# Turning the rotated keys and queries through memory, with all such transfers issued by GpSimd

## The chip, the cores and the metric

The kernel runs on one core of a Trainium2 chip. The metric is the device time of one execution in microseconds; lower is better. The core's engines run side by side, each working through its own list of instructions in order, and wait for one another on semaphores: TensorE (PE in the profile, PEld its weight loads) multiplies matrices and transposes 128x128 tiles, VectorE (DVE), ScalarE (ACT) and GpSimd (POOL) do elementwise work, SyncE (SP) issues the loads of the weights. Sixteen DMA engines move the data, whoever issues a transfer.

## The reference

One layer of an encoder for 256 tokens of width 2048, in float32. The part around the change is the attention branch: keys (4 heads) and queries (16 heads) of 128 channels are normalised per head, rotated, and used in a softmax over all tokens.

```python
q = rms_norm(q.reshape(b, s, ATTN_Q_HEADS, ATTN_HEAD_DIM), q_norm_g[layer])
k = rms_norm(k.reshape(b, s, ATTN_KV_HEADS, ATTN_HEAD_DIM), k_norm_g[layer])
v = v.reshape(b, s, ATTN_KV_HEADS, ATTN_HEAD_DIM)
q = apply_rope(q, cos, sin)
k = apply_rope(k, cos, sin)
y_attn = gqa_bidir_blocks(q, k, v)
...
branch_a = y_ssm @ w_ssm_up[layer]
branch_b = y_attn @ w_attn_up[layer]
merged = jax.nn.sigmoid(gate_a) * branch_a + jax.nn.sigmoid(gate_b) * branch_b
x = x + merged @ w_out[layer]
h2 = rms_norm(x, g_mlp[layer])
x = x + jnp.square(jax.nn.relu(h2 @ w_mlp_in[layer])) @ w_mlp_out[layer]
```

## The kernel before

The whole layer is a list of windows, written out in `walk`. A window multiplies the 256 tokens (two blocks of 128) by a 2048x512 slice of a weight matrix, in eight pieces p = 0 to 7 of 256 rows each. Every float32 product is made in three passes of a rounded high part and a low remainder, so a piece is 12 TensorE instructions of 512 columns. For each piece SyncE loads 128x1024 values into `raw`, ScalarE makes the high part `whi` (L653), VectorE the low part `wlo` (L1087), and TensorE uses both. `raw`, `whi` and `wlo` are rings of four pieces. ScalarE runs up to three pieces ahead of TensorE, VectorE two.

Behind each piece stands side work of the windows before, named in the last argument of `window(...)`: `rope` for a window of keys or queries, `attend` for the attention of one key head, and so on. Each engine has its own function of that name, called with the piece number p, and does its share in the order of the list, after its share of the piece. So whatever waits in a side function also holds up the high or low part of the following pieces on the same engine.

Several results have tokens in the partitions and are needed with channels in the partitions: they must be turned. Ten of these turns (four of `z`, three of `merged`, three of `residual`) go round TensorE: VectorE transposes 32x32 blocks into `blocks` (`turn_blocks`, L1125), ScalarE issues one transfer to the scratch rows `block_rows` in memory (`put_blocks`, L676), waits until it has landed and issues four transfers back into `turned_to` (`get_blocks`, L686), which place the blocks. ScalarE then makes the high part and VectorE the low part (`split_high`, `split_low`). Keys and queries go over TensorE instead: `rope` n = 0 is the keys and n = 1 to 4 the four groups of four query heads. At p = 6 TensorE waits for the rotated values in `tmp_a` and transposes eight tiles into the PSUM tensor `S` (`transpose_round`, L1834); at p = 7 ScalarE copies them as `kT_hi` or `qT_hi` (L919) and VectorE makes `kT_lo` or `qT_lo` (L1459).

The rotation itself takes VectorE and GpSimd: squares on ScalarE (L913), their sums on VectorE (L1428, L1431), an inverse root on GpSimd (L1716), the scaling on VectorE (L1440), then at p = 3 four multiplications by sines on GpSimd (L1770) and at p = 4 and 5 the multiplications by cosines and the additions on VectorE (L1451, L1454).

The windows around the change stand so in `walk`; (10, 1) and the like name a window by its row and half:

```python
window(10, 1, "v", 0, [("zturned", 3), ("rope", 0)])
window(11, 0, "q", 0, [("values", 0)])
window(11, 1, "q", 1, [("rope", 1)])
window(12, 0, "q", 2, [("rope", 2)])
window(12, 1, "q", 3, [("rope", 3)])
window(13, 0, "ssm_up", 0, [("attend", 0), ("rope", 4)])
window(13, 1, "ssm_up", 1, [("attend", 1), ("gated_a", 0)])
```

Within `attend` each of four heads h goes round all engines: scores on TensorE at p = h, maximum on VectorE, exponential on ScalarE, division on VectorE at p = h + 1 (L1475), transposes of the probabilities on TensorE at p = h + 3 (L1977), their high part `pT_hi` on ScalarE (L944) and low part `pT_lo` on VectorE (L1480) at the same p, and the product with the values on TensorE one piece later (L1813 to L1815, `S<-pT_hi,vg_hi`).

Of the kernel before, what the change touches and what calls it, by code (L numbers as in the profile page):

```python
# [65 lines left out]
BLOCK_ROUNDS = [rnd for rnd in range(TS_END) if rnd not in ON_PE]  # L66
# [3 lines left out]
def walk(eng, window):  # L70
# [194 lines left out]
def build(nc, x, x_t, w_in, w_dt, gains_in, taps_in, rows_in, w_ssm_up, w_attn_up, w_out, w_mlp_in, w_mlp_out,  # L265
# [129 lines left out]
    rden = place("rden", [P, 4, TB])  # L395
    assert top[0] <= nc.sbuf_usable_end, (top[0], nc.sbuf_usable_end)
# [3 lines left out]
    turned_to = nc.alloc_sbuf_tensor_at("turned_to", [P, 4, 4, TB, Q], F32, offset=region_r + 4 * TB * N)  # L400
    channels = nc.alloc_sbuf_tensor_at("channels", [P, 4, T], F32, offset=region_r + 8 * TB * N)
# [67 lines left out]
    r_sq, r_v, r_root, r_t, r_made = sem("r_sq"), sem("r_v"), sem("r_root"), sem("r_t"), sem("r_made")  # L469
# [82 lines left out]
    turned_wide = turned_to[:, :, :, :, :].rearrange("p i c b t -> p (c b) i t")  # L552

# [94 lines left out]
    def _(act):  # L648
# [22 lines left out]

        def put_blocks(rnd):

            d = BLOCK_ROUNDS.index(rnd)
            act.wait_ge(blocks_turned, d + 1)
            act.dma_start(block_rows[d], blocks[:, :, :, :, :].rearrange("p j c b t -> p (j c b t)")).then_inc(s_put, 16)  # L676

        def get_blocks(rnd):

            d = BLOCK_ROUNDS.index(rnd)  # L680
            act.wait_ge(s_put, 16 * (d + 1))
            if d:
                act.wait_ge(lined, d)
            rows = block_rows[d].rearrange("(i w) (j x) -> j w i x", i=4, j=4)
            for j in range(4):
                act.dma_start(turned_to[Q * j:Q * (j + 1), :, :, :, :].rearrange("w i c b t -> w i (c b t)"), rows[j]  # L686
                              ).then_inc(s_got, 16)
# [190 lines left out]
        def zgate(p, j, pr, pp):  # L878
# [90 lines left out]
        def merged(p, j, pr, pp):  # L969
            if j + TS_MERGED not in ON_PE and p == 1:  # L970
                put_blocks(j + TS_MERGED)
            if j + TS_MERGED not in ON_PE and p == 3:
                get_blocks(j + TS_MERGED)
            if p == (2 if j + TS_MERGED in ON_PE else 6):
                split_high(j + TS_MERGED, b_hi, j * 4, factor=0.5)

        def residual(p, j, pr, pp):
            if TS_X2 + j not in ON_PE and p == 1:
                put_blocks(TS_X2 + j)
            if TS_X2 + j not in ON_PE and p == 3:  # L980
                get_blocks(TS_X2 + j)
            if p == (2 if TS_X2 + j in ON_PE else 6):
                split_high(TS_X2 + j, a_hi, 4 * j, gain=1)
            if p == 2:
                for tb in range(TB):
                    act.activation(tmp_a[:, tb, :], x_sb[:, j, tb, :], ACT.Square,
                                   accum_out=rows_ss[:, tb, j:j + 1]).then_inc(sq_x, 1)
# [56 lines left out]
        table = {f.__name__: f for f in (rates, decays, conv, scan, gate, zgate, zturned, rope, values, attend, merged,  # L1044
# [39 lines left out]
    def _(dve):  # L1084
# [34 lines left out]
        def turn_blocks(rnd, src):  # L1119
# [4 lines left out]
            for tb in range(TB):  # L1124
                last = dve.transpose(blocks[:, :, :, tb, :].rearrange("p j c t -> p c j t"),  # L1125
# [289 lines left out]
        def zturned(p, j, pr, pp):  # L1415
            if p == 4:
                split_low(TS_Z + j, b_hi, b_lo, 4 * j, gain=2)

        def rope(p, n, pr, pp):
# [13 lines left out]
            if p == 2:  # L1433
                dve.wait_ge(r_root, 2 * (n + 1))
                if first(n):
                    dve.wait_ge(blocks_turned, TS_MERGED)
                else:
                    dve.wait_ge(r_t, n)
# [16 lines left out]
            if p == 7:  # L1455
                hi, lo = [t[:, 4 * n - 4:4 * n, :] for t in (qT_hi, qT_lo)] if n else (kT_hi, kT_lo)
                for c in range(2):
                    dve.wait_ge(r_made, 2 * n + c + 1)
                    dve.tensor_tensor(lo[:, 2 * c:2 * c + 2, :], S[:, c, :].rearrange("p (c t) -> p c t", c=2),  # L1459
                                      hi[:, 2 * c:2 * c + 2, :].bitcast(F32), ALU.subtract).then_inc(r_lo, 1)  # L1460
# [56 lines left out]
        def merged(p, j, pr, pp):  # L1517
            if p == 0:
                gated(4 + j, pr, pp)
                dve.wait_ge(taken[pp], pr + 1)  # L1520
                if j == 0:
                    dve.wait_ge(r_t, 5)
# [144 lines left out]
        table = {f.__name__: f for f in (rates, decays, conv, scan, tables, zgate, zturned, rope, attend, gated_a, merged,  # L1667
# [43 lines left out]
    def _(pool):  # L1711
# [36 lines left out]
        def zgate(p, j, pr, pp):  # L1748
            if p == 3:
                pool.wait_ge(z_v, j * Z_V + 3)  # L1750
                inverse_root(z_rs[:, :], z_rs[:, :], 4).then_inc(z_root, 1)

        def rope(p, n, pr, pp):
# [9 lines left out]
            if p == 3:  # L1763
                pool.wait_ge(taken[pp], pr + 1)
                pool.wait_ge(set_rope, 6)
                for tb in range(TB):
                    own = tmp_a[:, tb, :].rearrange("p (h d) -> p h d", h=4)
                    cross = tmp_b[:, tb, :].rearrange("p (h d) -> p h d", h=4)
                    for e in range(2):
# [3 lines left out]
                            ALU.mult).then_inc(r_cross, 1)  # L1773

# [9 lines left out]

# [476 lines left out]
```

## Time and profile before

| | before |
|---|---|
| median of 3 runs (lowest to highest) | 1618.38 us (1617.04 to 1618.45) |
| the profiled execution, its time | 1619.31 us |
| its span | 1617.5 us |
| granted clock of TensorE, mean over the span | 0.997 |
| TensorE busy | 1602.4 us (99%) |
| VectorE busy | 1273.3 us (79%) |
| ScalarE busy | 928.7 us (57%) |
| GpSimd busy | 79.7 us (5%) |

The profile is of one execution, and its own time lies 0.93 us above the median. Busy time is the union of an engine's instructions; matmuls overlap in it, so what one of them costs is the distance of the starts, not its duration. Times in the views are microseconds from the start of the span.

### The profile page before, as it was taken

How to read it: one execution, taken by the hardware profiler on the slowest of the kernel's cores; microseconds unless marked ns; L12 is line 12 of the kernel's file. 1: busy time of each engine (PE TensorE's matmuls, PEld its weight loads, DVE VectorE, ACT ScalarE, POOL GpSimd, SP SyncE). 2: the span in 40 equal slices, each digit the busy share in tenths (PEclk: the TensorE clock that was granted, in tenths of full speed). 3: DMA queues.
4: the chain of work that ended last, by engine and by line, in shares of the span. 5: the costliest groups of instructions: out<-in, count | busy, mean ns of one | idle time of the engine just before them, and what ended most of it. 6: DMA issues, size and time to landing. Idle time of an engine off the chain costs nothing.

```text
span 1617.5 us, 20663 instructions
## 1 busy us (share of the span) xinstructions
PE 1602.4 (99%) x8024; PEld 1355.1 (84%) x8024; DVE 1273.3 (79%) x1516; ACT 928.7 (57%) x1269; POOL 79.7 (5%) x67
## 2 busy tenths in 40 slices
PE   9999999999999999999999999999999999999998
PEld 7888888888888788888888888888888888888886
DVE  7978877888766677866665577999899988998793
ACT  6666556666565445544454655665556555655562
POOL 3000000000000133100000000000000000000000
PEclk9999999999999999999999999999999999999999
DMA  7665565666677665445787976458636764586471
GB/s 272 206 197 190 188 198 193 206 198 195 186 242 226 188 187 157 144 144 169 230 259 244 276 240 190 147 177 282 188 123 221 264 189 132 196 285 210 143 245 53
DMA packets 141393, 322.68 MB, mean 199 GB/s; under 512 B 10544, under 2 KB 16368, under 8 KB 141168
## 3 DMA queue, kind: packets, MB, share of 16 engines
q1 hardware_dynamic: 129376, 302.21, 58.1%
q10 hardware_dynamic: 11920, 19.17, 4.0%
q8 instruction: 63, 1.03, 0.3%
q14 instruction: 34, 0.28, 0.1%
HBM read 313.93 MB, written 7.41 MB: 199 GB/s over the span
## 4 chain that ended last, share of the span: by engine, by line
PE 88%; DVE 5%; DMA 3%; ACT 2%; issue 1%; ACTq 1%; POOL 0%; POOLq 0%; SPq 0%; DVEq 0%
PE G L1813 15%; PE G L1814 15%; PE G L1815 15%; PE G L1822 13%; PE S L1822 7%; PE G L1826 6%; PE S L1813 4%; PE S L1814 4%; PE S L1815 4%; PE S L1826 4%; DVE wlo L1087 1%; DMA block_rows<-blocks 1%; PE S L1940 1%; DMA raw<-in_w_out 1%; PE S L1834 1%
## 5 line engine op out<-in xcount | busy, mean ns | idle before, releaser
L653 ACT ACTIVATE whi<-raw 128x1024 fp32r<-128x1024 f32 x395 | 416.0, 1059 | 383.1 <-PE G L1815 213.7
L1087 DVE TENSOR_TENSOR wlo<-raw,whi 128x1024 fp32r<-128x1024 f32 x395 | 482.4, 1237 | 125.5 <-ACT whi L653 123.9
L1813 PE MATMUL G<-whi,a_both 128*128 128x512 f32 x768 | 300.9, 392 | 2.5 <-DVE wlo L1087 2.5
L1814 PE MATMUL G<-wlo,a_both 128*128 128x512 f32 x768 | 299.2, 390 | 0.0
L1815 PE MATMUL G<-whi,a_both 128*128 128x512 f32 x768 | 299.2, 390 | 0.0
L1822 PE MATMUL G<-a_both,whi 128*128 128x512 f32 x640 | 201.5, 396 | 0.0
L1813 PEld LDWEIGHTS G<-whi,a_both 128*128 128x128 f32 x768 | 144.6, 188 | 33.5 <-issue 1.9
L1815 PEld LDWEIGHTS G<-whi,a_both 128*128 128x128 f32 x768 | 144.3, 188 | 30.4
L1814 PEld LDWEIGHTS G<-wlo,a_both 128*128 128x128 f32 x768 | 144.4, 188 | 28.8
L1826 PEld LDWEIGHTS G<-a_both,wlo 128*128 128x128 f32 x640 | 120.2, 188 | 28.4
L1813 PE MATMUL G<-whi,b_hi 128*128 128x512 f32 x342 | 133.6, 391 | 0.0
L1814 PE MATMUL G<-wlo,b_hi 128*128 128x512 f32 x342 | 133.4, 390 | 0.0
L1815 PE MATMUL G<-whi,b_lo 128*128 128x512 f32 x342 | 133.1, 389 | 0.0
L653 ACT ACTIVATE whi_late<-raw 128x1024 fp32r<-128x1024 f32 x85 | 89.0, 1058 | 66.2 <-PE S L1826 22.3
L1826 PE MATMUL G<-a_both,wlo 128*128 128x256 f32 x640 | 125.8, 278 | 0.0
L1087 DVE TENSOR_TENSOR wlo_late<-raw,whi_late 128x1024 fp32r<-128x1024 f32 x85 | 102.5, 1221 | 23.5 <-ACT whi_late L653 23.2
L653 ACT ACTIVATE whi_late<-gates 128x1024 fp32r<-128x1024 f32 x67 | 70.0, 1056 | 51.7 <-PE G L1826 18.0
L1822 PEld LDWEIGHTS G<-a_both,whi 128*128 128x128 f32 x640 | 97.5, 189 | 0.1
L1087 DVE TENSOR_TENSOR wlo_late<-gates,whi_late 128x1024 fp32r<-128x1024 f32 x67 | 81.1, 1221 | 20.2 <-ACT whi_late L653 20.1
L653 ACT ACTIVATE whi<-gates 128x1024 fp32r<-128x1024 f32 x63 | 66.1, 1055 | 37.6 <-PE G L1826 13.9
L1087 DVE TENSOR_TENSOR wlo<-gates,whi 128x1024 fp32r<-128x1024 f32 x63 | 76.3, 1221 | 12.6 <-ACT whi L653 12.1
L1822 PE MATMUL G<-a_both,whi_late 128*128 128x512 f32 x256 | 80.4, 396 | 0.0
(313 smaller groups left out, 2696.8 us busy)
## 6 DMA issues: line engine op xcount, KB each, us to landing
raw<-in_w_in SPq DMA_DIRECT2D x208, 512.0 KB, 4.2
raw<-in_w_mlp_in SPq DMA_DIRECT2D x74, 512.0 KB, 4.5
raw<-in_w_mlp_out SPq DMA_DIRECT2D x74, 512.0 KB, 4.9
gates<-in_w_mlp_in SPq DMA_DIRECT2D x54, 512.0 KB, 4.1
gates<-in_w_mlp_out SPq DMA_DIRECT2D x54, 512.0 KB, 4.9
raw<-in_w_ssm_up SPq DMA_DIRECT2D x32, 512.0 KB, 3.8
raw<-in_w_attn_up SPq DMA_DIRECT2D x32, 512.0 KB, 4.7
raw<-in_w_out SPq DMA_DIRECT2D x32, 512.0 KB, 4.8
```

Of the source, the lines that this page charges most:

```text
L653: act.activation(high(m), piece(n), ACT.Copy).then_inc(hi_made, 1)
L1087: dve.tensor_tensor(low(m), piece(n), high(m).bitcast(F32), ALU.subtract).then_inc(lo_made, 1)
L1813: pe.matmul(out_ap, hi[:, k, cols], w_hi, start=start, stop=False)
L1814: pe.matmul(out_ap, hi[:, k, cols], w_lo, start=False, stop=False)
L1815: return pe.matmul(out_ap, lo[:, k, cols], w_hi, start=False, stop=stop)
L1822: pe.matmul(banks[:, c, :], high(m)[:, cols[kk]], a_both[:, 2 * p + kk, :, :].rearrange("p h t -> p (h t)"), start=(p + kk == 0), stop=False)
L1826: last = pe.matmul(banks[:, c, 0:T], low(m)[:, cols[kk]], a_hi[:, 2 * p + kk, :], start=False, stop=(2 * p + kk == KT - 1))
L1834: last = pe.transpose(S[:, c // 2, c % 2 * T + tb * P:c % 2 * T + (tb + 1) * P], src(c, tb), ident[:, :])
L1940: last = pe.matmul(S[:, 2, (4 * c + h) * HD:(4 * c + h + 1) * HD], mw[:, 0, h, c, :], tm[:, c, h * HD:(h + 1) * HD], start=True, stop=True)
```

## The change

The turns of keys and queries leave TensorE. VectorE turns 32x32 blocks at p = 6 of `rope`, GpSimd puts them into `block_rows` at p = 7, and a new side function `heads_in` n, one window later, brings them back: GpSimd issues the four transfers at p = 2, ScalarE makes the high part at p = 5, VectorE the low part at p = 6. Each of the five has buffers of its own for the blocks (`k_blocks`, `q_blocks`), and all five come back into `head_blocks`. `put_blocks` and `get_blocks` move from ScalarE to GpSimd for the ten older turns too, and for `z` the getting moves from p = 0 to 1, the high part from p = 3 to 5 and the low part from p = 4 to 6. TensorE's wait for a rotation is gone; `attend` g waits for the low parts that it needs. In the diff stand first the windows and then, in this order, the parts of ScalarE, VectorE, GpSimd and TensorE.

```diff
-BLOCK_ROUNDS = [rnd for rnd in range(TS_END) if rnd not in ON_PE]
+BLOCK_ROUNDS = [*range(TS_Z, TS_MERGED), *(("rope", n) for n in range(5)),
+                *(rnd for rnd in range(TS_MERGED, TS_END) if rnd not in ON_PE)]
...
-    window(11, 0, "q", 0, [("values", 0)])
+    window(11, 0, "q", 0, [("values", 0), ("heads_in", 0)])
     window(11, 1, "q", 1, [("rope", 1)])
-    window(12, 0, "q", 2, [("rope", 2)])
-    window(12, 1, "q", 3, [("rope", 3)])
-    window(13, 0, "ssm_up", 0, [("attend", 0), ("rope", 4)])
-    window(13, 1, "ssm_up", 1, [("attend", 1), ("gated_a", 0)])
+    window(12, 0, "q", 2, [("heads_in", 1), ("rope", 2)])
+    window(12, 1, "q", 3, [("heads_in", 2), ("rope", 3)])
+    window(13, 0, "ssm_up", 0, [("heads_in", 3), ("attend", 0), ("rope", 4)])
+    window(13, 1, "ssm_up", 1, [("heads_in", 4), ("attend", 1), ("gated_a", 0)])
...
-            if p == 6:
-                put_blocks(TS_Z + j)
-
         def zturned(p, j, pr, pp):
-            if p == 0:
-                get_blocks(TS_Z + j)
-            if p == 3:
+            if p == 5:
                 split_high(TS_Z + j, b_hi, 4 * j, gain=2)
...
-            if p == 7:
-                act.wait_ge(r_t, n + 1)
-                dst = qT_hi[:, 4 * n - 4:4 * n, :] if n else kT_hi
-                for c in range(2):
-                    act.activation(dst[:, 2 * c:2 * c + 2, :], S[:, c, :].rearrange("p (c t) -> p c t", c=2),
-                                   ACT.Copy).then_inc(r_made, 1)
+
+        def heads_in(p, n, pr, pp):
+            if p == 5:
+                d = BLOCK_ROUNDS.index(("rope", n))
+                act.wait_ge(s_got, 64 * (d + 1))
+                act.activation(by_block(head_parts(n)[0], 0, 4), heads_wide, ACT.Copy).then_inc(lined, 1)
...
+            if p == 6:
+                dve.wait_ge(r_v, (n + 1) * ROPE_V)
+                turn_blocks(("rope", n), tmp_a[:, :, :], rope_blocks(n))
+
+        def heads_in(p, n, pr, pp):
+            if p == 6:
+                hi, lo = head_parts(n)
+                dve.wait_ge(lined, BLOCK_ROUNDS.index(("rope", n)) + 1)
+                dve.tensor_tensor(by_block(lo, 0, 4), heads_wide, by_block(hi, 0, 4).bitcast(F32), ALU.subtract
+                                  ).then_inc(r_lo, 1)
...
+        def put_blocks(rnd, src=blocks[:, :, :, :, :]):
+
+            d = BLOCK_ROUNDS.index(rnd)
+            pool.wait_ge(blocks_turned, d + 1)
+            pool.dma_start(block_rows[d], src.rearrange("p j c b t -> p (j c b t)")).then_inc(s_put, 16)
+
+        def get_blocks(rnd, dst=turned_to):
+
+            d = BLOCK_ROUNDS.index(rnd)
+            pool.wait_ge(s_put, 16 * (d + 1))
+            if d:
+                pool.wait_ge(lined, d)
+            rows = block_rows[d].rearrange("(i w) (j x) -> j w i x", i=4, j=4)
+            for j in range(4):
+                pool.dma_start(dst[Q * j:Q * (j + 1), :, :, :, :].rearrange("w i c b t -> w i (c b t)"), rows[j]
+                              ).then_inc(s_got, 16)
...
+        def heads_in(p, n, pr, pp):
+            if p == 2:
+                if n:
+                    pool.wait_ge(r_lo, n)
+                get_blocks(("rope", n), head_blocks)
...
-        def rope(p, n, pr, pp):
-            if p == 6:
-                pe.wait_ge(r_v, (n + 1) * ROPE_V)
-                if n == 0:
-                    pe.wait_ge(scan_v, SCAN_V * GROUPS)
-                else:
-                    pe.wait_ge(r_lo, 2 * n)
-                if n == 4:
-                    pe.wait_ge(at_exp, 8)
-                transpose_round(lambda c, tb: tmp_a[:, tb, c * P:(c + 1) * P]).then_inc(r_t, 1)
-
         def attend(p, g, pr, pp):
             def scores(h):
-                pe.wait_ge(r_lo, 2 * (5 if g else 4))
+                pe.wait_ge(r_lo, g + 2)
+                if (g, h) == (0, 0):
+                    pe.wait_ge(scan_v, SCAN_V * GROUPS)
```

Two lists show where the moved instructions stand now. The first place is on ScalarE, from the last piece but a few of window (10, 0) into window (10, 1), where `rope` 0 begins; `L653` (`L668` after the change) is the high part of a weight piece, `b_hi` that of `z`. Before:

```order
L706 ACTIVATE b_hi<-channels 128x1024
L653 ACTIVATE whi<-raw 128x1024 x3
L676 DMA block_rows<-blocks 128x1024
L653 ACTIVATE whi<-raw 128x1024 x2
L686 DMA turned_to<-block_rows 32x4x256 x4
L913 ACTIVATE tmp_b<-G,rstd 128x512 x2
L653 ACTIVATE whi<-raw 128x1024 x3
```

And with the change:

```order
L704 ACTIVATE b_hi<-channels 128x1024
L668 ACTIVATE whi<-raw 128x1024 x3
L906 ACTIVATE tmp_b<-G,rstd 128x512 x2
L668 ACTIVATE whi<-raw 128x1024 x5
L700 ACTIVATE channels<-turned_to,gains 128x256 x4
```

The put and the four gets no longer stand ahead of the squares of `rope` 0, and the reading of `turned_to` has moved two pieces back.

The second place is window (13, 0), where `attend` 0, `rope` 4 and now `heads_in` 3 meet. On GpSimd before, from the inverse root of `rope` 4 to the values of `attend` 1:

```order
L1716 TENSOR_TENSOR q_rs<-q_rs,minus_half 128x8
L1759 TENSOR_TENSOR q_rs<-q_rs,rstd 128x8
L1770 TENSOR_TENSOR tmp_b<-tmp_a,rope_t 128x256 x4
L1780 CAST vg_hi<-v_sb 128x256
L1782 TENSOR_TENSOR vg_lo<-v_sb,vg_hi 128x256
```

And with the change:

```order
L1703 TENSOR_TENSOR q_rs<-q_rs,minus_half 128x8
L1748 TENSOR_TENSOR q_rs<-q_rs,rstd 128x8
L1790 DMA head_blocks<-block_rows 32x4x256 x4
L1759 TENSOR_TENSOR tmp_b<-tmp_a,rope_t 128x256 x4
L1780 DMA block_rows<-q_blocks_131 128x1024
L1771 CAST vg_hi<-v_sb 128x256
L1773 TENSOR_TENSOR vg_lo<-v_sb,vg_hi 128x256
```

Four transfers now stand ahead of the multiplications by sines, and the put ahead of the values of `attend` 1.

On VectorE the same window from p = 5 to the last piece, before:

```order
L1087 TENSOR_TENSOR wlo<-raw,whi 128x1024
L1480 TENSOR_TENSOR pT_lo<-S,pT_hi 128x512
L1487 TENSOR_TENSOR a_both<-S,a_both 128x2x256
L1451 TENSOR_TENSOR tmp_a<-tmp_a,rope_t 128x512
L1454 TENSOR_TENSOR tmp_a<-tmp_a,tmp_b 128x512
L1087 TENSOR_TENSOR wlo<-raw,whi 128x1024
L1480 TENSOR_TENSOR pT_lo<-S,pT_hi 128x512
L1087 TENSOR_TENSOR wlo<-raw,whi 128x1024
L1487 TENSOR_TENSOR a_both<-S,a_both 128x2x256
L1459 TENSOR_TENSOR qT_lo<-S,qT_hi 128x512 x2
```

And with the change:

```order
L1073 TENSOR_TENSOR wlo<-raw,whi 128x1024
L1467 TENSOR_TENSOR pT_lo<-S,pT_hi 128x512
L1474 TENSOR_TENSOR a_both<-S,a_both 128x2x256
L1434 TENSOR_TENSOR tmp_a<-tmp_a,rope_t 128x512
L1437 TENSOR_TENSOR tmp_a<-tmp_a,tmp_b 128x512
L1073 TENSOR_TENSOR wlo<-raw,whi 128x1024
L1446 TENSOR_TENSOR qT_lo<-head_blocks,qT_hi 128x1024
L1467 TENSOR_TENSOR pT_lo<-S,pT_hi 128x512
L1111 STREAM_TRANSPOSE q_blocks_131<-tmp_a 128x4x4x32 x2
L1073 TENSOR_TENSOR wlo<-raw,whi 128x1024
L1474 TENSOR_TENSOR a_both<-S,a_both 128x2x256
```

The low part of the queries stands ahead of the last `pT_lo` of the window, and the block transposes behind it.

## Rows read from the trace of the kernel before

**Rows 1.** Page, first part: busy time and share of TensorE and its weight loads.

```profile
PE 1602.4 (99%) x8024; PEld 1355.1 (84%) x8024; DVE 1273.3 (79%) x1516; ACT 928.7 (57%) x1269; POOL 79.7 (5%) x67
```

**Rows 2.** Waits of TensorE, 430 to 960 us: total, times, longest.

```profile
PE S L1834 <- DVE tmp_a L1454: 3.0, 2, 2.8
PE G L1813 <- DVE wlo L1087: 0.7, 1, 0.7
```

**Rows 3.** Timeline of TensorE round the turn of the keys: start, duration, instruction.

```profile
533.72 0.39 PE L1815 MATMUL G<-whi,a_both 128*128 128x512 f32 x1
536.95 1.97 PE L1834 MATMUL S<-ident,tmp_a 128*128 128x128 f32 x8 [2.84 <-DVE tmp_a L1454]
...
540.00 0.40 PE L1813 MATMUL G<-whi,a_both 128*128 128x512 f32 x1
```

**Rows 4.** Stretches: PE, PEld, DVE, ACT, POOL busy (count), PE clock, DMA share, GB/s.

```profile
537.00:538.60 1.60, 1.60 (x9) 1.60 (x9) 1.60 (x2) 0.00 (x0) 0.00 (x0) 0.50 0.76 289
538.60:547.70 9.10, 9.10 (x39) 7.49 (x38) 5.44 (x6) 4.36 (x6) 0.00 (x0) 0.92 0.74 230
```

**Rows 5.** Timeline of TensorE round two later turns, `rope` 1 and `rope` 4.

```profile
582.65 0.39 PE L1815 MATMUL G<-whi,a_both 128*128 128x512 f32 x1
582.88 1.03 PE L1834 MATMUL S<-ident,tmp_a 128*128 128x128 f32 x8
...
584.45 0.40 PE L1813 MATMUL G<-whi,a_both 128*128 128x512 f32 x1
...
658.19 1.09 PE L1834 MATMUL S<-ident,tmp_a 128*128 128x128 f32 x8 [0.18 <-DVE tmp_a L1454]
```

**Rows 6.** Timelines of ScalarE and TensorE in window (10, 1).

```profile
520.60 1.27 ACT L913 ACTIVATE tmp_b<-G,rstd 128x512 f32<-128x512 f32 x2 [5.41 <-issue]
...
528.37 0.50 PE L1813 MATMUL G<-whi,a_both 128*128 128x512 f32 x1 [0.73 <-DVE wlo L1087]
```

**Rows 7.** Lines L676 and L686: issue ns min/median/max, then us to landing.

```profile
DMA to landing us min/median/max: 2.7/3.2/6.4
L686 ACTq DMA_DIRECT2D turned_to<-block_rows x40: 309/453/1286, 448.9 to 914.6; - x40
DMA to landing us min/median/max: 3.2/5.6/8.3
```

**Rows 8.** Lines L1125 and L1133: duration ns min/median/max, first and last start.

```profile
L1125 DVE STREAM_TRANSPOSE blocks<-tmp_a x8: 666/686/705, 440.2 to 510.4; 128x512 f32<-128x512 f32 x8
L1133 DVE TENSOR_TENSOR b_lo<-channels,b_hi x7: 1225/1226/1872, 461.1 to 839.2; 128x1024 fp32r<-128x1024 f32 x7
```

**Rows 9.** The busiest window of queries as a stretch, columns as in rows 4.

```profile
574.00:597.00 23.00, 23.00 (x107) 19.10 (x107) 17.82 (x20) 10.62 (x12) 7.81 (x7) 1.00 0.63 187
```

**Rows 10.** Timeline of GpSimd in window (13, 0).

```profile
642.00 2.61 POOL L1716 TENSOR_TENSOR q_rs<-q_rs,minus_half 128x8 f32<-128x8 f32 x1 [17.35 <-DVE q_rs L1431]
...
646.29 4.25 POOL L1770 TENSOR_TENSOR tmp_b<-tmp_a,rope_t 128x256 f32<-128x256 f32 x4 [1.40 <-DVE tmp_a L1440]
```

**Rows 11.** Timeline of ScalarE in window (13, 0), p = 5.

```profile
650.82 1.06 ACT L653 ACTIVATE whi<-raw 128x1024 fp32r<-128x1024 f32 x1
654.21 0.60 ACT L944 ACTIVATE pT_hi<-S 128x512 fp32r<-128x512 f32 x1 [2.33 <-PE S L1815]
```

**Rows 12.** Timeline of VectorE in window (13, 0).

```profile
648.85 1.84 DVE L1475 TENSOR_SCALAR prob<-prob,rden 128x256 f32<-128x256 f32 x2
...
655.53 0.68 DVE L1480 TENSOR_TENSOR pT_lo<-S,pT_hi 128x512 fp32r<-128x512 f32 x1
...
659.19 0.68 DVE L1480 TENSOR_TENSOR pT_lo<-S,pT_hi 128x512 fp32r<-128x512 f32 x1
```

**Rows 13.** Line L1475: duration ns min/median/max, first and last start.

```profile
L1475 DVE TENSOR_SCALAR prob<-prob,rden x32: 346/352/983, 639.9 to 741.7; 128x256 f32<-128x256 f32 x32
```

**Rows 14.** Timeline of TensorE: products with the values of heads 2 and 3.

```profile
657.04 0.37 PE L1813 MATMUL S<-pT_hi,vg_hi 128*128 128x256 f32 x1
...
661.90 0.28 PE L1813 MATMUL S<-pT_hi,vg_hi 128*128 128x256 f32 x1
```

More of the change, by code:

```diff
@@ L395, in build @@
     rden = place("rden", [P, 4, TB])
+    head_blocks = place("head_blocks", [P, 4, 4, TB, Q])
     assert top[0] <= nc.sbuf_usable_end, (top[0], nc.sbuf_usable_end)
@@ L670, in split @@
             high_part(m, n)
[L672 to L687, printed above, removed]
         def split_high(rnd, dst, k0, gain=None, factor=1.0):
@@ L984, in residual @@
             if p == 2:
+                act.wait_ge(taken[pp], pr + 1)
                 for tb in range(TB):
@@ L1042, in finish @@
                     final_squares(j, tb)
-        table = {f.__name__: f for f in (rates, decays, conv, scan, gate, zgate, zturned, rope, values, attend, merged,
+        table = {f.__name__: f for f in (rates, decays, conv, scan, gate, zgate, zturned, rope, heads_in, values, attend, merged,
                                          residual, hidden, finish)}
@@ L1124, in turn_blocks @@
             for tb in range(TB):
-                last = dve.transpose(blocks[:, :, :, tb, :].rearrange("p j c t -> p c j t"),
+                last = dve.transpose(dst[:, :, :, tb, :].rearrange("p j c t -> p c j t"),
                                      src[:, tb, :].rearrange("p (c j w) -> p c j w", c=4, w=Q))
@@ L1665, in finish @@
                     times_gain(j, tb)
-        table = {f.__name__: f for f in (rates, decays, conv, scan, tables, zgate, zturned, rope, attend, gated_a, merged,
+        table = {f.__name__: f for f in (rates, decays, conv, scan, tables, zgate, zturned, rope, heads_in, attend, gated_a, merged,
                                          residual, hidden, sums, mixed, mix_out, finish)}
@@ L1783, in attend, with zturned, merged @@
                                    ).then_inc(vg_made, 1)
+        def put_blocks(rnd, src=blocks[:, :, :, :, :]):
[11 more added lines that the diff above has]
+                              ).then_inc(s_got, 16)
+        def zturned(p, j, pr, pp):
+            if p == 1:
+                get_blocks(TS_Z + j)
+        def heads_in(p, n, pr, pp):
[3 more added lines that the diff above has]
+                get_blocks(("rope", n), head_blocks)
+        def merged(p, j, pr, pp):
+            if j + TS_MERGED not in ON_PE and p == 1:
+                put_blocks(j + TS_MERGED)
+            if j + TS_MERGED not in ON_PE and p == 3:
+                get_blocks(j + TS_MERGED)
         def residual(p, j, pr, pp):
+            if TS_X2 + j not in ON_PE and p == 1:
+                put_blocks(TS_X2 + j)
+            if TS_X2 + j not in ON_PE and p == 3:
+                get_blocks(TS_X2 + j)
             if p == 4 and j == 3:
@@ L1788, in residual @@
                 inverse_root(rstd_mlp[:, :], x_var[:, :], TB).then_inc(rstd_x, 1)
-        table = {f.__name__: f for f in (rates, scan, zgate, rope, attend, residual)}
+        table = {f.__name__: f for f in (rates, scan, zgate, zturned, rope, heads_in, attend, merged, residual)}
         def window(r, par, kind, idx, sides):
@@ L2014, in residual @@
                 last.then_inc(row_mm, 1)
-        table = {f.__name__: f for f in (rates, decays, conv, scan, rope, attend, merged, residual)}
+        table = {f.__name__: f for f in (rates, decays, conv, scan, attend, merged, residual)}
         def last_window(r, par, idx):
```

41 lines of the change are left out of this document (19 added, 22 removed).

## The prediction

> **What bounds the kernel now.** I read the page first: TensorE is busy for 1602.4 of 1617.5 us [rows 1]. So the end moves only by what TensorE no longer executes, or no longer waits for, and by new waits of its own. I then asked for its waits alone, from 430 to 960 us: it waits 3.0 us for rotated values (L1454) ahead of a turn and 0.7 us for the low part of a weight piece (L1087) [rows 2]. The timeline gives the price of a turn. Products follow one another every 0.23 us (582.65 to 582.88) [rows 5], so a piece of 12 lasts 2.76 us. The granted clock shows one more thing: behind the idle 2.84 us of the first turn it is 0.50, the lower level of 1.2 GHz, from 537.0 to 538.6 us and 0.92 on average over the 9.1 us that follow [rows 3, 4]. That is 1.6 us and another 9.1 x 0.08 / 0.5 = 1.5 us at half speed, which lose half of 3.1, about 1.5 us.
>
> **What goes.** Each of the five turns is eight transposes.
>
> First turn (keys): the fourth product behind it starts at 540.00 us, and the last ahead of it started at 533.72 [rows 3]. Four steps of 0.23 would have taken 0.92 us, it took 6.28, so 5.36 us go. In them lie the wait of 2.84 and the 1.5 us of the slow clock.
>
> Second, third and fourth (the first three groups of queries): 584.45 - 582.65 - 0.92 = 0.88 us [rows 5]; the other two look alike, so 3 x 0.88 = 2.64 us.
>
> Fifth: the same and an idle 0.18 us [rows 5], 1.06 us.
>
> The transfers' move away from ScalarE frees one more wait. In window (10, 1) ScalarE stood for 5.41 us in front of L913, because the put of the last `z` had to land before the gets could be issued; the high parts behind it came late, and TensorE waited 0.73 us for `wlo` at 528.37 [rows 6]. With the change nothing of a transfer stands on ScalarE there, so these 0.73 us go too.
>
> Sum: 5.36 + 2.64 + 1.06 + 0.73 = 9.79 us.
>
> **What comes, and what hides it.** VectorE gets a block transpose per turn, 2 x 0.69 us, and one low part of 1.23 us where it had two halves from PSUM [rows 8]; the latter I count as equal. That is 5 x 1.37 = 6.9 us more work. Its cover: in the busiest window of queries VectorE works 17.82 of 23 us [rows 9], so 19.2 of 23 with it; without that cover a window would grow by up to 1.4 us. On ScalarE one high part of 1024 columns (1.06 us, as for a weight piece [rows 11]) replaces two from PSUM, at nothing.
>
> The transfers are 25 more (five puts, 20 gets), and all 75 are now issued by GpSimd. No row shows a transfer that GpSimd issues. By ScalarE a get takes 0.45 us to issue and lands 3.2 to 8.3 us later, median 5.6; a put lands after 2.7 to 6.4 [rows 7]. Below, I take GpSimd as fast as that; above, that each transfer can also be held as long as GpSimd's or VectorE's instructions hold one another. How long that is shows L1475: it normally takes 0.352 us and at most 0.983, and the pair at 648.85 takes 1.84 us while GpSimd multiplies from 646.29 to 650.54 [rows 10, 12, 13], so more than a microsecond can go in one meeting; the longest VectorE instruction about here takes 1.23 [rows 8]. I take 1 us per transfer, near the lower end, since most of VectorE's work is the subtraction of weights and not L1475.
>
> For the turns of `z` the read lies four pieces (11.0 us) behind the get. Those of `merged` and `residual` are put as soon as VectorE has turned at p = 0 and read at p = 6, six pieces or 16.6 us later; put, issues and get need 3.2 + 5 x 1 + 5.6 = 13.8. For keys and the first two query groups, ScalarE may wait in `heads_in` for about 7 us: the piece that it owes next is used four pieces (11.0 us) after it begins with the last one; less that one's 1.06 us, the next one's 1.06 and VectorE's 1.23, 7.6 are left. Cost nothing.
>
> The narrow place is window (13, 0). GpSimd is done with the inverse root at 644.6 and a short scaling at about 644.9 [rows 10]. Then come the four gets, which end at 648.9 by my 1 us each, and the last lands at 652.1 to 654.5 (3.2 to 5.6 later). ScalarE comes to `heads_in` 3 at 651.9 and did `pT_hi` of head 2 at 654.21 [rows 11]; with the high part of 1.06 us it will do it at 654.2 to 655.6. VectorE's low part stood at 655.53, TensorE's product at 657.04 [rows 12, 14], so up to 0.8 us of that are free. Head 3 is tighter. TensorE's product stood at 661.90; without the fifth turn it wants to start at 660.84. VectorE ended `pT_lo` at 659.87 and now has 1.23 us ahead of it: 661.1, so 0.3 us late. The four multiplications on GpSimd start about 4 us later than 646.29 and so meet other instructions of VectorE (L1475 at p = 4, then L1451 and L1454); one meeting of about a microsecond makes it 1.2 us in all. In window (13, 1) `heads_in` 4 has more room (no inverse root and no multiplications on GpSimd): 0. New waits: 1.2 us, between 0 and about 4.
>
> **The sum.** 9.79 - 1.2 = 8.6 us. The profiled execution took 1619.31 us and would take 1610.7; the median of the runs is 0.93 below it, which gives **1609.8 us**.
>
> **A rule that speaks against it.** The row first: the pair L1475 at 1.84 us instead of 0.70 [rows 12, 13]. The Trainium skill, "SBUF — State Buffer", section "SBUF: two separate sides", says that VectorE and GpSimd lock a shared pair of ports for a whole instruction, and that a transfer issued by GpSimd then waits for its descriptors to be written, 3100 ns instead of 620 in its example; the section "Who interferes with whom" counts `tensor_scalar` among the instructions that lock, and `tensor_tensor` not against writes. L1475 is such a `tensor_scalar`, and the row agrees. By that page's example each of the five transfers of a turn could come 2.5 us later, an estimate; what that would give is the second case below.
>
> **The rivals.**
>
> *GpSimd late in the attention (1614).* Each get waits for a VectorE instruction (0.45 + 1.23 us): the four end at 651.6, the last lands 5.6 later at 657.2, `pT_hi` of head 2 comes at 658.3, `pT_lo` at 659.6 instead of the 657.0 that TensorE wants. That is 2.6 us, and as behind the first turn an idle stretch of this length may bring 1.5 us of slow clock: 4.1, and with a landing of 8.3 us 6.8. So 1619.31 - 9.79 + 5.5 - 0.93 = 1614. For it: 1 us per transfer is my choice, not a row. Against: four meetings in a row are much.
>
> *Transfers so late that ScalarE stops at nearly every read (1624).* This is the case on the other side. The six turns of `merged` and `residual` have 16.6 us and about 7 more before TensorE stands; by ScalarE's prices they need 3.2 + 5 x 0.45 + 5.6 = 11.1. It decides from (16.6 + 7 - 11.1) / 5 = 2.5 us more per transfer. At that point window (13, 0) alone has its gets issued by 644.9 + 4 x 2.95 = 656.7, landed at 662.3, `pT_lo` of head 2 at 664.6: 7.6 us lost, time 1616. At 3 us more it is 2 us worse there, and the six turns lose 5 x 0.5 = 2.5 us each: 1633. I put it in the middle. Against it: nothing in the rows holds GpSimd for 2.5 us, the longest meeting being about a microsecond [rows 12, 13]. The rule above, at 2.5 us, reaches just this point.
>
> *The time is not given back (1617.5).* VectorE, 6.9 us busier, makes TensorE wait for `wlo` instead: five windows by 1.4 us give 6.9, and 1618.38 - 8.6 + 6.9 is about 1617. Against it: 3.8 us per window stay free.
>
> *Cheaper still (1608.6).* No new wait at all: 1619.31 - 9.79 - 0.93 = 1608.6.
>
> **How the numbers follow.** The forecast has 0.57, GpSimd late in the attention 0.18, transfers late everywhere 0.10, not given back 0.07, cheaper 0.08. A measurement of this kernel tells about 0.2% from no change, 3.2 us: faster is below 1615.1. Faster: 0.57 + 0.08 + 0.13 of the 0.18 = 0.78; within: 0.05 + 0.07 = 0.12; slower 0.10. The range of 1607.5 to 1616.0 takes in the lower bound, the forecast and the late attention, and leaves out some 2 in 10. The forecast's own range is 1608 to 1612.
>
> **What would show it.** Right: no L1834 between 500 and 700 us, the granted clock at 1.00 from 530 to 560, no wait for `wlo` at 528, ScalarE without an idle 5.4 us in front of the squares of the keys; in window (13, 0) a TensorE wait for `pT_lo` of about 1 us. Wrong: idle time of ScalarE that ends with `turned_to` or `head_blocks`, above all at p = 5 of (13, 0); VectorE instructions longer than their median while GpSimd issues; landing times far above 5.6 us; TensorE waits for `wlo` at `merged` and `residual`.

## The result, and the profile after

The changed kernel took 1636.78 us (median of 4 runs, 1634.56 to 1637.77) beside 1618.41 us of the kernel before: a ratio of 1.0111, 95% interval 1.0092 to 1.0130. It is slower by 18.4 us; the forecast was 8.6 us faster. The profiled execution has a span of 1634.1 us, for 1617.5 before.

The page's first part and TensorE's waits from 430 to 960 us, which answer to [rows 1, 2]:

```profile
PE 1604.9 (98%) x7984; PEld 1354.5 (83%) x7984; DVE 1278.0 (78%) x1521; ACT 927.0 (57%) x1264; POOL 118.0 (7%) x142
```

```profile
PE G L1841 <- DVE wlo L1073: 6.9, 5, 2.8
PE S L1862 <- DVE gates L1529: 5.4, 1, 5.4
PE S L1862 <- DVE tmp_b L1516: 2.8, 1, 2.8
PE S L1841 <- DVE wlo L1073: 2.1, 1, 2.1
PE S L1841 <- DVE pT_lo L1467: 0.4, 1, 0.4
PE S L1996 <- DVE pT_lo L1467: 0.2, 1, 0.2
```

TensorE has 40 instructions less, the five turns, and waits 17.8 us in this stretch. Before it had waited 4.1: the 3.7 of [rows 2] and one wait of 0.4 us that they leave out:

```profile
PE S L1834 <- DVE tmp_b L1529: 0.4, 1, 0.4
```

Around the new waits TensorE's clock also falls. Stretches of the changed kernel, with TensorE's busy time (count), granted clock, DMA share and GB/s: one whole part of the kernel first, then the five falls.

```profile
430.00:600.00 170.00, 170.00 (x752) 1.00 0.74 227
622.70:626.10 3.40, 3.40 (x8) 0.52 0.49 154
820.00:823.40 3.40, 3.40 (x9) 0.58 0.46 154
847.30:850.70 3.40, 2.33 (x10) 0.58 0.48 144
919.00:922.40 3.40, 3.40 (x10) 0.58 0.58 188
946.30:949.70 3.40, 2.31 (x10) 0.58 1.03 381
```

Five stretches at nearly the lower level of 1.2 GHz lose at most 3.4 x (0.48 + 4 x 0.42) = 7.3 us, where one of 1.5 us had been [rows 3, 4]. It is an upper bound, since in two of them TensorE is busy for only 2.3 of the 3.4 us and the rest is counted with the waits. Each lies beside an idle stretch of 2.1 to 5.4 us. The balance of the spans: 17.8 - 4.1 = 13.7 us more of waits, up to 5.8 more of slow clock, less five turns of 0.88 us = 4.4: up to 15.1 of the measured 16.6 us.

Why it waits is told by the line of the four gets, L1790. A get is one transfer back from memory; the four of a turn are issued in a loop. Duration in ns (min/median/max), what GpSimd's idle time before it ended with, who waited for it, and the time to landing:

```profile
L1790 POOL DMA_DIRECT2D turned_to<-block_rows x40: 552/553/583, 447.9 to 933.4; - x40
L1790 POOL DMA_DIRECT2D head_blocks<-block_rows x20: 552/553/617, 538.2 to 668.0; - x20
  issue: 87.0, 19
  DMA block_rows<-blocks: 36.0, 10
  ACT channels L700: 12.1, 3
  ACT channels L697: 10.8, 3
  ACT qT_hi L913: 6.2, 3
  ACT kT_hi L913: 1.2, 1
DMA to landing us min/median/max: 2.7/4.7/8.4
```

A get takes 0.55 us to issue (0.62 at most), and lands as soon as one of ScalarE did: a median of 4.7 us after its issue, for 5.6 [rows 7]. What is new is 87.0 us of "issue", idle time of GpSimd that the profile puts to nothing, and 30.3 us of stops of ScalarE. The timeline of GpSimd shows where the idle time stands, in all fifteen turns alike; here in a residual turn and in window (13, 0):

```profile
897.63 1.70 POOL L1790 DMA_DIRECT2D turned_to<-block_rows  x3 [2.92 <-DMA block_rows<-blocks]
907.55 0.55 POOL L1790 DMA_DIRECT2D turned_to<-block_rows  x1 [8.22 <-issue]
...
640.47 1.72 POOL L1790 DMA_DIRECT2D head_blocks<-block_rows  x3 [0.31 <-issue]
644.75 0.56 POOL L1790 DMA_DIRECT2D head_blocks<-block_rows  x1 [2.56 <-issue]
```

Three gets leave in a row, the fourth comes 2.6 to 8.2 us later. The same line from 898.6 to 899.6 us alone, which takes in the second and third get of the first of these turns:

```profile
L1790 POOL DMA_DIRECT2D turned_to<-block_rows x2: 552/557/562, 898.2 to 898.8; - x2
DMA to landing us min/median/max: 7.0/7.7/8.4
```

The third is issued at 898.8 and lands after 8.4 us, at 907.2; the fourth is issued at 907.55. In window (13, 0) the third lands at 641.6 + 2.8 = 644.4, and the fourth follows at 644.75. So the fourth leaves 0.3 to 0.4 us after the third has landed. It is so in all fifteen turns (0.31 to 0.37 us), and the landing of the first get, 1.0 to 3.3 us before that of the third, lets nothing leave. The fourth lands itself 2.7 to 5.4 us after its issue.

The data of a turn is then late. ScalarE, VectorE and TensorE behind the second and third residual turn:

```profile
912.97 1.71 ACT L700 ACTIVATE channels<-turned_to,gains 128x256 f32<-128x256 f32 x4 [5.84 <-DMA turned_to<-block_rows]
...
938.68 1.71 ACT L700 ACTIVATE channels<-turned_to,gains 128x256 f32<-128x256 f32 x4 [4.75 <-DMA turned_to<-block_rows]
```

```profile
941.51 1.23 DVE L1119 TENSOR_TENSOR a_both<-channels,a_both 128x1024 fp32r<-128x1024 f32 x1 [6.33 <-ACT a_both L704]
942.65 2.35 DVE L1073 TENSOR_TENSOR wlo<-raw,whi 128x1024 fp32r<-128x1024 f32 x2
944.92 1.22 DVE L1073 TENSOR_TENSOR wlo_late<-gates,whi_late 128x1024 fp32r<-128x1024 f32 x1
946.06 1.28 DVE L1529 TENSOR_TENSOR gates<-gates,S 128x512 f32<-128x512 f32 x2
```

```profile
947.39 1.97 PE L1862 MATMUL S<-ident,gates 128*128 128x128 f32 x8 [5.36 <-DVE gates L1529]
```

ScalarE stops 4.75 us, VectorE behind it 6.33 us, and it then has three weight pieces to catch up on before the sums that TensorE wants to turn: 5.36 us of idle TensorE, the longest wait of the kernel. The eight transposes take 1.97 us instead of 1.09 at the lower clock.

A second path leads from the fourth get to TensorE, in window (12, 1). GpSimd, then VectorE, then TensorE:

```profile
616.37 0.55 POOL L1790 DMA_DIRECT2D head_blocks<-block_rows  x1 [4.98 <-issue]
616.93 3.27 POOL L1759 TENSOR_TENSOR tmp_b<-tmp_a,rope_t 128x256 f32<-128x256 f32 x4
```

```profile
618.73 2.03 DVE L1434 TENSOR_TENSOR tmp_a<-tmp_a,rope_t 128x512 f32<-128x512 f32 x1 [5.04 <-POOL tmp_b L1759]
```

```profile
622.68 0.80 PE L1841 MATMUL G<-whi,a_both 128*128 128x512 f32 x1 [2.84 <-DVE wlo L1073]
```

The multiplications by the sines stand behind the waiting get on GpSimd, VectorE stops 5.04 us for them, and the low part of a weight piece behind that is late.

### The profile page after: what moved, and what is told of

It reads as the page before. It is cut to its first block, busy times and chain, and to the rows that moved or that the text cites. A ratio compares the mean times of both kernels' runs of the same rounds, so it can differ in the third digit from the quotient of the medians.

```text
span 1634.1 us, 20614 instructions
## 1 busy us (share of the span) xinstructions
PE 1604.9 (98%) x7984; PEld 1354.5 (83%) x7984; DVE 1278.0 (78%) x1521; ACT 927.0 (57%) x1264; POOL 118.0 (7%) x142
## 4 chain that ended last, share of the span: by engine, by line
PE 82%; issue 12%; DMA 2%; DVE 2%; POOL 1%; ACT 1%; POOLq 0%; ACTq 0%; DVEq 0%
PE G L1841 13%; PE G L1842 13%; PE G L1843 13%; PE G L1850 13%; PE S L1850 7%; PE G L1854 6%; PE S L1854 4%; PE S L1841 3%; PE S L1842 3%; PE S L1843 3%; DMA block_rows<-blocks 1%; PE S L1968 1%; POOL turned_to L1790 1%; DVE wlo L1073 1%; DMA raw<-in_w_in 0%
## 5 line engine op out<-in xcount | busy, mean ns | idle before, releaser
L668 ACT ACTIVATE whi<-raw 128x1024 fp32r<-128x1024 f32 x395 | 415.0, 1058 | 386.4 <-PE G L1843 197.3
L668 ACT ACTIVATE whi_late<-raw 128x1024 fp32r<-128x1024 f32 x85 | 88.9, 1058 | 67.1 <-PE S L1854 22.3
L668 ACT ACTIVATE whi_late<-gates 128x1024 fp32r<-128x1024 f32 x67 | 70.0, 1056 | 50.9 <-PE G L1854 18.7
L668 ACT ACTIVATE whi<-gates 128x1024 fp32r<-128x1024 f32 x63 | 66.1, 1056 | 38.5 <-PE G L1854 13.9
```

What stands on the lines that cost most here:

```text
L668: act.activation(high(m), piece(n), ACT.Copy).then_inc(hi_made, 1)
```

## The experiments

Both kernels are built with `dynamic_dma_scratch_size=512`. The Trainium skill, "DMA: Bandwidth & Descriptors", section "SWDGE vs HWDGE vs iDMA", says that GpSimd writes the descriptors of its transfers into rings in a set-aside part of SBUF, and ScalarE's transfers use none; I took this number for the size of that part, and it was the first suspect. Before the change no transfer was GpSimd's. One line of the change that the diff leaves out, a wait of ScalarE in `residual` at p = 2 (`act.wait_ge(taken[pp], pr + 1)`), stands in all the runs at 384 to 768 bytes alike, so it does not set them apart. The medians of the kernel before, in the runs of the same chips, are 1619.42 us (first four experiments), 1617.06 (next four) and 1618.0 (last three); each ratio is to these.

**768 bytes for the descriptors.** The changed kernel with

```
-    dynamic_dma_scratch_size=512
+    dynamic_dma_scratch_size=768
```

> The changed kernel with only the descriptor scratch raised from 512 to 768 bytes. Theory A (the ring is full: three gets issue in 1.7 us and the fourth waits 4.3 to 8.2 us for the first to land): the fourth get follows at once, the waits of ScalarE for turned_to go, 1608.5 to 1612 us. Theory B (VectorE's instructions hold up GpSimd's writing of descriptors): the scratch's size changes nothing, 1634 to 1638 us. Theory C (VectorE's extra work makes wlo late): also 1634 to 1638.

Measured: 1615.41 us, ratio 0.9976 (0.9966 to 0.9987): against the changed kernel's 1.0111, by this number alone. The gets of GpSimd, idle time first:

```profile
  issue: 4.6, 4
DMA to landing us min/median/max: 2.8/5.7/10.1
```

All four leave in a row, in 2.2 us; 87.0 us of "issue" are 4.6, and ScalarE's stops for turned data, 30.3 us, are 1.2. That settles theory A as the cause of the loss; only what the fourth get waits for is not as A has it, the landing of the third and not of the first. The time lies 3 us above the top of A's range, and TensorE's longest wait had a new place, the last of these rows (VectorE, GpSimd, TensorE):

```profile
639.38 2.96 DVE L1455 TENSOR_SCALAR nb<-mx 128x2 f32<-128x2 f32 x1
```

```profile
636.80 2.26 POOL L1790 DMA_DIRECT2D head_blocks<-block_rows  x4 [0.51 <-issue]
639.08 3.22 POOL L1759 TENSOR_TENSOR tmp_b<-tmp_a,rope_t 128x256 f32<-128x256 f32 x4
```

```profile
643.08 0.63 PE L1996 MATMUL S<-ident,prob 128*128 128x128 f32 x4 [2.71 <-DVE rden L1459]
```

An instruction on 128 x 2 elements, 0.17 us everywhere else, took 2.96 us: it ended when GpSimd's four multiplications did, and `rden`, for which TensorE waited, stands behind it on VectorE. Behind it the granted clock was 0.76 from 643 to 650 us. Two experiments below are on that.

**384 bytes.** The other way.

> The changed kernel with the scratch cut from 512 to 384 bytes. Theory A: only two gets of a turn find room at once, the third and the fourth each wait for a landing, so the last get comes another 3 to 6 us later and the kernel takes 1645 to 1665 us. Theories B and C: as the changed kernel, 1634 to 1638.

Measured: 1641.56 us, ratio 1.0134 (1.0118 to 1.0150), 5 us above 512 bytes: less than expected. GpSimd in the same residual turn:

```profile
902.05 1.11 POOL L1790 DMA_DIRECT2D turned_to<-block_rows  x2 [3.17 <-DMA block_rows<-blocks]
910.48 1.10 POOL L1790 DMA_DIRECT2D turned_to<-block_rows  x2 [7.32 <-issue]
```

Two leave, then two: one wait per turn, not two, so the last get is hardly later than at 512. In all fifteen turns the third get leaves 0.28 to 0.38 us after the landing of the second, the last one in flight, and the fourth goes with it. By these times the full place opens for both at once, where A had it opening get by get and so overrated the loss.

**640 bytes** (in the last group of runs).

> The changed kernel with 640 bytes for GpSimd's descriptors instead of 512. At 384 bytes two reads of each round left in a row and two waited, at 512 three and one, at 768 all four. Theory A (the place holds so many reads, 128 bytes each): at 640 all four leave in a row, and the time is that of 768 bytes, 1615.4 us (1613 to 1618). Rival W (the write of the round also still holds its place): the fourth read waits in some of the rounds, 1618 to 1630.

Measured: 1612.88 us, ratio 0.9971 (0.9961 to 0.9982); a little below the 1613 to 1618 expected. All fifteen turns leave four gets in a row, and no stop of ScalarE for turned data is left. Theory A holds in its count: two, three and four gets in a row at 384, 512 and 640 bytes, and nothing more from 768. The 2.5 us wait for `rden` is there too. Rival W is not excluded by this, though: at 128 bytes each, 512 bytes would hold four, and only three left. Either one place stays free or the put of the turn still fills one; four gets and a put also come to 640 bytes. No run tells the two apart.

**Only the ten older turns by GpSimd, 512 bytes.** The kernel before, with `put_blocks` and `get_blocks` on GpSimd and the parts of `z` moved as in the change, and the five turns of keys and queries left to TensorE (code shortened):

```
-            act.dma_start(block_rows[d], blocks[...]).then_inc(s_put, 16)
+            pool.dma_start(block_rows[d], blocks[...]).then_inc(s_put, 16)
...
-                act.dma_start(turned_to[...], rows[j]).then_inc(s_got, 16)
+                pool.dma_start(turned_to[...], rows[j]).then_inc(s_got, 16)
```

> The kernel before with only the ten older turns moved to GpSimd; keys and queries stay on TensorE. Theory A: nearly the whole loss sits in the six turns of merged and residual, so slower than before by 14 us of waits and about 7 us of slow clock: 1636 to 1642 us. Theory C (the heads are at fault): about 1618, within 2 us of before.

Measured: 1634.06 us, ratio 1.0093 (1.0073 to 1.0113), 14.6 us slower, 2 us less than theory A gave. So most of the loss has nothing to do with keys and queries: it comes from the ten turns that worked before. The fourth get waits here too, in all ten turns.

**The same with 768 bytes.**

> The kernel before, with its ten older turns alone issued by GpSimd, and 768 bytes. With 512 bytes it stood at 1634.06 us, and ScalarE waited 18.9 us for the last reads. Theory A (the loss of these ten turns is all the fourth read's): it comes back to the kernel before, 1617 to 1620 us, since the runs of 1611.17 and 1609.2 us, which differ in who issues the ten turns, put at most 2 us on it. Rival T (a read by GpSimd costs more in itself, 0.55 us for 0.45 on ScalarE, and lands later): 1623 to 1630 us.

Measured: 1616.77 us, ratio 0.9996 (0.9986 to 1.0007), where 1617 to 1620 us was expected. ScalarE's stops for turned data are down from 18.9 us to 0.6. Rival T falls. With room for the descriptors it makes no difference whether ScalarE or GpSimd issues these ten.

**Only the five turns of keys and queries by GpSimd, 512 bytes.** The changed kernel, with the older turns issued by ScalarE at their old pieces, on semaphores of their own (code shortened):

```
-            pool.dma_start(block_rows[d], src...).then_inc(s_put, 16)
+            pool.dma_start(block_rows[d], src...).then_inc(h_put, 16)
...
-        def merged(p, j, pr, pp):     (in GpSimd's program; back in ScalarE's)
```

> The changed kernel with the ten older turns back on ScalarE at their old pieces; keys and queries go through memory by GpSimd, with semaphores of their own. Theory A: TensorE is spared 9.1 us of turns and pays the 3 to 4 us of waits and up to 1.7 us of slow clock that the changed kernel shows between 500 and 700 us: 1612 to 1616 us. Theory C: 1630 or more.

Measured: 1616.3 us, ratio 0.9975 (0.9962 to 0.9989), 0.3 us above the 1612 to 1616 expected. A small gain, although the fourth get waits here as well. The second path told above costs the most, 3.38 us; waits of 1.48 and 0.81 us for `wlo` stand at 536 and 602 us:

```profile
622.22 0.56 POOL L1825 DMA_DIRECT2D head_blocks<-block_rows  x1 [5.13 <-issue]
...
624.60 2.02 DVE L1471 TENSOR_TENSOR tmp_a<-tmp_a,rope_t 128x512 f32<-128x512 f32 x1 [5.27 <-POOL tmp_b L1794]
...
628.53 0.50 PE L1862 MATMUL G<-whi,a_both 128*128 128x512 f32 x1 [3.38 <-DVE wlo L1110]
```

**768 bytes, multiplications ahead of the gets in window (13, 0).** There the gets of the fourth query turn are issued behind the multiplications (and ScalarE and VectorE take that turn a piece later):

```
         def heads_in(p, n, pr, pp):          (GpSimd)
-            if p == 2:
+            if p == (3 if n == 3 else 2):    (called at the end of rope's p == 3)
```

> The kernel with 768 bytes for GpSimd's descriptors stood at 1615.41 us; its longest wait of TensorE (2.71 us, for rden at 643.08) followed an nb of two elements that lay 2.96 us on VectorE while GpSimd made its four multiplications by the sines; the clock fell for 3.4 us behind it. Here, in window (13,0) alone, the multiplications come before the four reads of the fourth query turn, so that they start some 2.3 us sooner; ScalarE and VectorE take that turn one piece later. Theory M (the reads on GpSimd pushed the multiplications onto nb): nb takes 0.2 to 0.8 us, the wait of 2.7 us goes, and the fall of the clock behind it with its 1.7 us: 1611.0 us (1610 to 1612.5). Rival N (VectorE is held wherever the multiplications lie, the place doesn't matter): another instruction of VectorE is held 1.5 to 3 us and TensorE waits as before: 1614.5 to 1616.

Measured: 1611.17 us, ratio 0.9968 (0.9956 to 0.9979). GpSimd and VectorE:

```profile
637.14 4.26 POOL L1759 TENSOR_TENSOR tmp_b<-tmp_a,rope_t 128x256 f32<-128x256 f32 x4 [1.40 <-DVE tmp_a L1423]
641.34 2.29 POOL L1792 DMA_DIRECT2D head_blocks<-block_rows  x4
```

```profile
638.83 0.17 DVE L1455 TENSOR_SCALAR nb<-mx 128x2 f32<-128x2 f32 x1
```

The wait is gone, and in the profiled execution (span 1607.2 us, the fastest of the twelve) the clock is 1.00 from 600 to 960 us. But `nb` takes 0.17 us here in the middle of GpSimd's multiplications, which take 4.26 us instead of 3.22. So "meets the multiplications" is not the whole condition: `nb` was held when it began 0.3 us after their start, and not 1.7 us after, as in the kernel before too. Another instruction is held in its place, as rival N had it: the pair L1462 takes 1.85 us instead of 0.62. But TensorE does not wait for it, so the place matters. As a time, the step from 0.9976 to 0.9968 is 1.3 us on two chips, with intervals that overlap, and not the 4.4 forecast; a cleaner pair comes below.

**Only keys and queries, 768 bytes, gets first; and the same with the multiplications first.**

> Only the five turns of keys and queries on GpSimd, with 768 bytes, and the reads ahead of the multiplications as in the changed kernel; the run with the multiplications first stood at 1609.2 us. Theory M (in window (13,0) the reads push the multiplications onto an nb of VectorE): nb takes 2 to 3 us there, TensorE waits some 2.7 us and its clock falls: 1613.6 us (1611.5 to 1614.5). Rival (with the older turns on ScalarE the window has other times, and they miss each other, as at 512 bytes): 1609.2 us (1608 to 1611).

Measured: 1613.31 us, ratio 0.9971 (0.9961 to 0.9980). `nb` again:

```profile
639.30 2.95 DVE L1492 TENSOR_SCALAR nb<-mx 128x2 f32<-128x2 f32 x1
```

It was held 2.95 us, TensorE waited 2.70, and its granted clock was 0.76 from 643 to 650 us: theory M, as forecast.

> The kernel that has only the five turns of keys and queries on GpSimd and the ten older ones on ScalarE (1616.3 us with 512 bytes), with 768 bytes and the multiplications ahead of the fourth query's reads in window (13,0). At 512 bytes its fourth read lay 5.13 us on GpSimd at 622.22, the multiplications came behind it, VectorE stopped 5.27 us for them and TensorE 3.38 us. Theory A (it is the fourth read at 512 bytes): the 3.38 us go, and no other wait above 1 us comes: 1612.5 us (1611 to 1614). Rival S (moving the five turns gives nothing in itself, the work on ScalarE takes it back): 1616 us, as before.

Measured: 1609.2 us, ratio 0.9956 (0.9941 to 0.9972), the fastest of all, below both kernels and 2 us below the forecast range. TensorE's waits from 430 to 960 us are down to

```profile
PE S L1885 <- DVE tmp_b L1553: 0.6, 1, 0.6
PE G L1864 <- DVE wlo L1110: 0.2, 1, 0.2
```

By the ratios the multiplications first are worth 0.0015, 2.4 us, again on two chips and with intervals that overlap.

**768 bytes, gets of the merged and residual turns held back.** One line ahead of each:

```
+                pool.wait_ge(hi_made, split_so_far[0])
                 get_blocks(j + TS_MERGED)
```

> The kernel with 768 bytes and one edit: for the merged and the residual turns GpSimd's four reads wait until ScalarE has made as many high parts as it had when ScalarE issued these reads itself. Theory P (the unpaced reads, 3.4 us sooner at 821, come between the loads of x and of the weights): the waits of TensorE for wlo (1.89 us at 834) and for gates (0.73 us at 930) go, with the fall of the clock behind the first: 1611.1 us (1610 to 1613). Rival Q (the loads of weights are late there by SyncE's own order: three loads of x of 512 KB each are issued 3.7 us sooner than in the kernel before, and no read of GpSimd is in their way): no change, 1614.5 to 1616.

Measured: 1617.36 us, ratio 1.0006 (0.9996 to 1.0017): worse, not better. Theory P falls, and its ground was a misreading: the gets came 3.4 us sooner than in the kernel before because everything did by then. From the put to the gets it is 3.75 us with 768 bytes (817.62 to 821.37), as it was on ScalarE. TensorE's wait for `wlo` at 834 us was 2.65 us here, not gone.

**Both edits.**

> Both edits of the two runs beside it in one kernel. Theories M and P together: 1615.4 less 4.4 and 4.3 us, 1606.7 us (1605.5 to 1609). M alone: 1611 us. P alone: 1611 us. Neither: 1615 us.

Measured: 1613.99 us, ratio 0.9983 (0.9971 to 0.9994): none of the four values forecast. Against the run above on the same chip the multiplications first give 3.4 us, with intervals apart, where the trace of that run had 2.71 us of wait for `rden` and no fall of the clock behind it: this is the clean pair for theory M. Against the multiplications first without the hold (1611.17, the same chip) the hold costs 2.8 us; the ratios' intervals overlap a little, but of the twelve times of each kernel only the extremes meet (up to 1613.52, from 1613.07). It did act in three of the six turns; one of them, its gets 6.7 us behind their put:

```profile
866.00 2.19 POOL L1792 DMA_DIRECT2D turned_to<-block_rows  x4 [6.16 <-ACT whi L668]
```

So holding the gets back costs time there, even by 1 to 3 us. How they reach TensorE stays open; its waits are again those near 834 us, where the loads of `x` and of the weights come together. These waits differed between kernels whose code is the same there (1.9 us, 0.7 and 0.2 in three of them), and that was not run down.

## Why the prediction was wrong, point by point

**What bounds the kernel now**: right. TensorE's waits and its clock make up some 15 of the 16.6 us.

**What goes**, 9.79 us: right in kind, probably too large. Nothing of L1834 is left, the clock is 1.00 from 430 to 600 us, the waits at 528 and 536 us are gone. Where the new waits are taken away (768 bytes, multiplications first), 0.8 and 0.7 us of waits are left, so some 9 us should be gained. The spans of the profiled executions are 8.9 and 10.3 us below 1617.5; but the profiled 1619.31 us lies above most medians of the kernel before, and by the medians the gains are 7.1 us (ratio 0.9956) and 5.2 us (0.9968). The 2 to 4 us between were not run down. In the changed kernel the gain was outweighed.

**What comes: the price of a transfer by GpSimd.** This is the step that failed: "I take 1 us per transfer". A get costs 0.55 us, below my figure, and none of the 60 took more than 0.62. But a price per transfer was the wrong form. The cost sits in the fourth get of a turn, which waits for the landing of the third, 2.6 to 8.2 us, when the place for descriptors has 512 bytes. I bounded the price by how long instructions of GpSimd and VectorE hold one another, and did not ask what GpSimd's queue has that ScalarE's has not; the number 512 stood in the kernel, unused until this change. The runs at 384, 512, 640 and 768 bytes show the cause. That the last landing in flight is what lets the next get leave was read off the times, 15 turns at 384 bytes and 30 at 512, and not tested apart; how the place is emptied stays open.

**The cover of the merged and residual turns**, "need 13.8 of 16.6, cost nothing": failed by the same step. From the put at 894.16 us (3.47 ahead of the gets at 897.63) ScalarE had its data at 912.97, 18.8 us later. And the "about 7 more before TensorE stands" were not there: a stop of ScalarE of 5.84 us cost TensorE 2.08, and one of 4.75 cost it 5.36. That room was worked out for the window of the keys, with weight pieces ready; here VectorE owed three low parts and the loads of weights were late as well.

**Window (13, 0)**: right at the start. GpSimd's order pushed the multiplications by the sines later, VectorE's low part of the queries stood ahead of `pT_lo`, and TensorE waited 0.4 and 0.2 us for `pT_lo`, where the forecast had 0.3 us and a meeting of about a microsecond. The low part took 1.22 us, the block transposes 0.69, as counted. The meeting of about a microsecond was with L1475 in the forecast; with room for the descriptors it was `nb`, for 2.96 us, and cost 2.7 us and a fall of the clock.

**The rule that speaks against it.** The 60 gets of the changed kernel lie between 552 and 617 ns, while VectorE is busy for 78% of the span; nothing of VectorE's held a transfer of GpSimd. The delay to 3100 ns that the Trainium skill ("SBUF — State Buffer", "SBUF: two separate sides") tells of is not seen here. It was hardly put to the test either: the gets met mostly `tensor_tensor` instructions, and none met the scaling (L1462, L1475 before), the `tensor_scalar` from which I had my figure. In the run at 384 bytes a pair of gets did, at 641.87 us, and took 1.20 us instead of 1.10. The rule that bore on this case is the one of the Trainium skill, "DMA: Bandwidth & Descriptors", "SWDGE vs HWDGE vs iDMA", of rings that GpSimd writes; the runs agree with it, since the size of the part alone moved the time.

**The rivals.** "Transfers so late that ScalarE stops at nearly every read" named the right symptom (ScalarE stops for `turned_to` and `head_blocks` in ten places, TensorE waits at merged and residual) and the right sign. Its condition, 2.5 us more per transfer or some 10 per turn, was not met: 2.6 to 8.2 us per turn did it. Its 1624 is too low still: the place where it decides was worked out with the 7 us of room. "GpSimd late in the attention" is what only the keys and queries at 512 bytes show, and it costs 3.4 us in window (12, 1), not in (13, 0). "The time is not given back" shows nowhere in the trace: VectorE's extra work fitted, TensorE was busy for 170.00 of 170 us up to 600 us.

## What to carry to other kernels

When a transfer moves to GpSimd, ask how many it has in flight at once and how large the place for its descriptors is: here four gets of 128 KB in a row needed 640 bytes, and at 512 each turn lost 2.6 to 8.2 us. In a trace it shows as idle time put to "issue" between two transfers of one loop, which ends just after the last one in flight lands, while each transfer keeps its normal duration. And slack must be worked out at every place that relies on it: one number for it, 7 us from the window where all is ready, did not hold where weights were late too, where stops of 5.84 and 4.75 us cost TensorE 2.08 and 5.36.

## What the runs showed of the hardware that I had not expected

- Transfers of GpSimd in a row, by bytes set aside: 2 at 384, 3 at 512, 4 at 640 and 768, for gets of 128 KB. The next one leaves 0.3 to 0.4 us after the landing of the last one in flight, and not when the first lands.
- With room, who issues makes no difference in time: ten turns by GpSimd or by ScalarE gave a ratio of 0.9996 (0.9986 to 1.0007), though a get takes 0.55 us of GpSimd and 0.45 of ScalarE.
- A VectorE instruction on 128 x 2 elements was held 2.96, 2.95 and 2.78 us (0.17 otherwise) when it began 0.3 to 0.5 us after the first of four multiplications of GpSimd, until the last had ended; begun 1.7 us after, it took 0.17, a pair on 128 x 256 elements took 1.85 us instead of 0.62, and the four took 1 us longer.
- In the changed kernel each idle stretch of TensorE of over 2 us had one of 3.4 us at a granted clock of 0.52 to 0.58 beside it. It is no rule: behind idle stretches of 3.38 us (keys and queries alone, 512 bytes, 628.5 to 638 us) and of 2.71 (the held gets, 643 to 650 us) the granted clock was 1.00.
